# Three feed-forwards of a two-block model: who makes the low halves of the first six weight blocks, and when

## The reference, cut to what matters

```
def swiglu(h, w13, w2):
    gate, up = jnp.split(h @ w13, 2, axis=-1)
    return (jax.nn.silu(gate) * up) @ w2

x = x + 0.5 * swiglu(rms_norm(x, g), w13, w2)      # six times, D_FF = 2816
x = x + token_mixer(rms_norm(x, g), ...)           # pooling, HGRN, RWKV-7 and GLA heads, then y @ w_out
x = x + rglru_block(rms_norm(x, g), ...)           # conv, gates, linear recurrence, then y @ w_out
x = x + stick_breaking_block(rms_norm(x, g), ...)  # attention, then o @ w_o
```

## Time and profile before

| what | value |
|---|---|
| median of three runs | 1563.62 us |
| span of the profiled execution | 1561.3 us |
| TensorE, weight loads | 1536.0 us (98%), 1335.9 (86%) |
| VectorE, ScalarE, GpSimd | 1078.8 (69%), 776.3 (50%), 982.8 (63%) |
| mean DMA | 169 GB/s |

### The profile page before, as it was taken

One profiled execution on the slowest core, in us unless ns is written; L12 is line 12 of the kernel. 1 busy time (PEld: TensorE's weight loads), 2 busy tenths in 40 slices (PEclk: granted clock), 3 DMA queues, 4 the chain that ended last, 5 costly groups with the idle time before them and its releaser, 6 DMA issues.

```text
span 1561.3 us, 25169 instructions
## 1 busy us (share of the span) xinstructions
PE 1536.0 (98%) x9772; PEld 1335.9 (86%) x9772; DVE 1078.8 (69%) x1451; ACT 776.3 (50%) x1118; POOL 982.8 (63%) x1154
## 2 busy tenths in 40 slices
PE   9999999999999999999999999999999999999998
PEld 7888887887788888888998788888888888878887
DVE  7866555756886668976579886656776655688664
ACT  6454442023555465554666555455555454665542
POOL 7966520202886677876774886676977671288764
PEclk9999999999999999999999999999999999999999
DMA  8665533222465564565636466564465561336553
GB/s 294 204 195 184 187 109 109 75 90 97 166 210 188 169 199 158 191 202 183 195 132 189 145 210 190 168 223 139 156 224 181 166 229 55 134 121 222 182 167 120
DMA packets 107206, 263.69 MB, mean 169 GB/s; under 512 B 9168, under 2 KB 43088, under 8 KB 106960
## 3 DMA queue, kind: packets, MB, share of 16 engines
q1 hardware_dynamic: 107088, 262.09, 51.0%
HBM read 261.00 MB, written 1.05 MB: 168 GB/s over the span
## 4 chain that ended last, share of the span: by engine, by line
PE 83%; POOL 7%; DVE 6%; ACT 2%; issue 1%; DMA 0%; SPq 0%; DVEq 0%; ACTq 0%
PE ps L1739 38%; PE ps L1740 21%; POOL w_lo L543 7%; PE ps L1787 6%; PE ps L1742 4%; PE ps L1833 2%; PE ps L1771 2%; PE ps L1773 1%; PE ps L1772 1%; PE ps L1854 1%; PE ps L2046 1%; PE ps L1941 1%; DVE xn L1023 1%; PE ps L1803 1%; DVE arena L1680 1%
## 5 line engine op out<-in xcount | busy, mean ns | idle before, releaser
L543 POOL TENSOR_TENSOR w_lo<-raw,w_hi 128x256 fp32r<-128x256 f32 x1120 | 964.1, 895 | 463.0 <-ACT w_hi L625 460.1
L1739 PE MATMUL ps<-xn,w_hi 128*128 128x512 f32 x1848 | 662.0, 397 | 11.0 <-POOL w_lo L543 5.2
L625 ACT ACTIVATE w_hi<-raw 128x1024 fp32r<-128x1024 f32 (+1 forms) x518 | 477.7, 933 | 175.3 <-PE ps L1742 100.4
L1740 PE MATMUL ps<-xn,w_lo 128*128 128x256 f32 x2112 | 550.3, 280 | 0.0
L1739 PEld LDWEIGHTS ps<-xn,w_hi 128*128 128x128 f32 x1848 | 346.4, 187 | 94.3 <-POOL w_lo L543 8.4
L1740 PEld LDWEIGHTS ps<-xn,w_lo 128*128 128x128 f32 x2112 | 398.4, 189 | 16.8
L1739 PE MATMUL ps<-hid,w_hi 128*128 128x512 f32 x1008 | 363.4, 396 | 1.2 <-DVE w_lo L1015 1.2
L1015 DVE TENSOR_TENSOR w_lo<-raw,w_hi 128x512 fp32r<-128x512 f32 (+1 forms) x232 | 269.4, 1161 | 35.6 <-ACT w_hi L625 30.4
L1740 PE MATMUL ps<-hid,w_lo 128*128 128x256 f32 x1056 | 292.4, 281 | 0.0
L1739 PEld LDWEIGHTS ps<-hid,w_hi 128*128 128x128 f32 x1008 | 190.1, 189 | 42.5 <-issue 1.5
L1099 DVE TENSOR_TENSOR arena<-ps,low_part 128x512 f32<-128x512 f32 x132 | 90.8, 688 | 179.2 <-ACT low_part L716 179.0
(11 more groups left out here) (334 smaller groups left out, 1496.1 us busy)
## 6 DMA issues: line engine op xcount, KB each, us to landing
raw<-blocks SPq DMA_DIRECT2D x419, 512.0 KB, 3.6
raw<-blocks SPq DMA_DIRECT2D x144, 256.0 KB, 3.6
cst<-consts SPq DMA_DIRECT2D x1, 2358.0 KB, 14.9
x<-x_in SPq DMA_DIRECT2D x4, 256.0 KB, 5.4
out<-x SPq DMA_DIRECT2D x4, 256.0 KB, 3.3
cst<-consts SPq DMA_DIRECT2D x1, 109.0 KB, 2.1
```

The costliest lines, as they stand in the source:

```text
L543: ins = nc.gpsimd.tensor_tensor(w_lo[:, slot(n), piece], raw[:, slot(n), piece], w_hi[:, slot(n), piece], ALU.subtract)
L625: nc.scalar.activation(w_hi[:, slot(n), cols], raw[:, slot(n), cols], ACT.Copy)\
L1739: nc.tensor.matmul(where, hi, both.rearrange("p a t -> p (a t)"), start=opens, stop=False)
L1740: ins = nc.tensor.matmul(where[:, 0:SEQ], lo, high, start=False, stop=False)
```

## The change

In words: in front of `ffn_b`, `ffn_d` and `ffn_f` (`BEHIND_ROWS`) GpSimd makes the low halves of blocks 0, 1 and 5, VectorE those of 2 and 3 before its first sum of x and that of 4 behind the squares; VectorE's additions of squares move behind all sums of x and low halves. ScalarE has a norm of its own there: the high halves of blocks up to 3 (`ffn_b`) or 4 (`ffn_d`, `ffn_f`) are made ahead of the first sum, in the mixer those of 0 and 1 ahead of a wait; squares come one pair later, and the high halves up to block 5 right behind them. GpSimd takes the low halves of rows 4 and 5 of `lru_out` from VectorE. At the start there are 7 of the old unused products and 16 others in fp32r, for which VectorE fills a part of `hid` with ones. `ffn_a`, `ffn_c` and `ffn_e` keep their order.

```diff
-UNUSED_PRODUCTS = 11
+UNUSED_PRODUCTS = 7
+BEHIND_ROWS = {"ffn_b": "mix_out", "ffn_d": "lru_out", "ffn_f": "attn_out"}
+POOL_ROWS = (4, 5)
+def first_on_vector(phase):
+    return DVE_SPLITS if phase == "ffn_a" else (2, 3, 4) if phase in BEHIND_ROWS else ()
...
@@ GpSimd
+                if phase == "lru_out":
+                    for i in POOL_ROWS:
+                        lo(n0 + i)
...
-                    for n in range(n0, n0 + 2 * LEAD):
-                        if n not in DVE_SPLITS:
-                            lo(n)
+                    for i in range(2 * LEAD):
+                        if i not in first_on_vector(phase):
+                            lo(n0 + i)
@@ ScalarE
+            def norm_behind_rows(version, phase, gains):
+                n0 = FIRST[phase]
+                def square(a):
+                    nc.scalar.activation(squares(a, gains), pair_of_x(a), ACT.Square).then_inc(sq_ready, 1)
+                for a in range(4):
+                    act.wait_ge(x_ready, 4 * (version - 1) + a + 1)
+                    high_halves(gains, a)
+                    if a:
+                        square(a - 1)
+                square(3)
+                hi_until(n0 + 2 * LEAD - 1)
+                preload(ACT.Sqrt)
+                state["norms"] += 1
+                take_low(FFN_OF[gains], n0, 0)
...
@@ ScalarE, mixer_one
                 inverse_root(rms_r[:, :, :], bank(4), HD, const("gn_eps"), "rw_gn_root")
+                hi_until(FIRST["ffn_b"] + 1)
                 need(act, "on_done", 2)
                 inverse_root(norm_sb[:, 0, :], bank(6)[:, 0, :], G, const("norm_eps"), "on_root")
-                hi_until(FIRST["ffn_b"] + 2)
+                hi_until(FIRST["ffn_b"] + 3)
@@ ScalarE, lru and attention
-                hi_until(out_rows + 8 + 2)
+                hi_until(FIRST["ffn_d"] + 4)
...
-                hi_until(FIRST["ffn_f"] + 2)
+                hi_until(FIRST["ffn_f"] + 4)
@@ VectorE
+            def next_x(scale, gains, rows, following):
+                n0 = FIRST[following]
+                def add(a):
...
+                before, behind = first_on_vector(following)[:2], first_on_vector(following)[2:]
+                for i in before:
+                    lo(n0 + i)
+                add(0)
+                add(1)
+                low_halves(gains, 0)
+                add(2)
+                low_halves(gains, 1)
+                add(3)
+                low_halves(gains, 2)
+                low_halves(gains, 3)
+                for a in range(4):
+                    add_squares(a, gains)
+                for i in behind:
+                    lo(n0 + i)
                 sums_done[0] += 1
                 inverse_root(gains)
@@ VectorE, lru
                     y_low("lru_out", lru_gate, i)
-                    lo(FIRST["lru_out"] + i)
+                    if i not in POOL_ROWS:
+                        lo(FIRST["lru_out"] + i)
@@ VectorE, start
-            nc.vector.memset(low_part[:, :, :], 1.0).then_inc(ones_ready, 1)
+            nc.vector.memset(low_part[:, :, :], 1.0)
+            nc.vector.memset(hid[:, 0:2, :, :].bitcast(F32), 1.0).then_inc(ones_ready, 1)
@@ TensorE, start
+            unused_both = hid[:, 0, :, :].rearrange("p a t -> p (a t)")
+            for _ in range(4):
+                nc.tensor.matmul(ps[:, 7, 0:SEQ], hid[:, 0, 0, 0:P], hid[:, 0, 1, :], start=True, stop=True)
+            for _ in range(3):
+                nc.tensor.matmul(ps[:, 7, :], hid[:, 0, 0, 0:P], unused_both, start=True, stop=True)
+            for _ in range(3):
+                nc.tensor.matmul(ps[0:HD, 7, 0:SEQ], hid[:, 0, 0, 0:HD], hid[:, 0, 1, :], start=True, stop=True)
+            for _ in range(3):
+                nc.tensor.matmul(ps[:, 7, 0:SEQ], hid[0:HD, 0, 0, 0:P], hid[0:HD, 0, 1, :], start=True, stop=True)
+            unused_apart = hid[:, 0:2, :, :].rearrange("p c a t -> p (c a) t")[:, :, 0:P]
+            for _ in range(3):
+                nc.tensor.matmul(ps[:, 7, :], hid[:, 0, 0, 0:P], unused_apart, start=True, stop=True)
```

More of the change, by code:

```diff
@@ L636, in preload, with norm @@
                 chain(nc.scalar.activation(table[:, 0:4], table[:, 4:8], func))
-            def norm(version, gains, then=ACT.Silu, after=None, late=(), behind=None):
+            def norm(version, gains, then=ACT.Silu, after=None, behind=None):
                 for a in range(4):
@@ L678, in norm @@
                     preload(then)
+            def norm_behind_rows(version, phase, gains):
[12 more added lines that the diff above has]
+                take_low(FFN_OF[gains], n0, 0)
+                act.wait_ge(total_ready, state["norms"])
+                nc.scalar.activation(rms[:, :], ps[:, 3, 0:SEQ], ACT.Sqrt, scale=1.0 / D, bias=const("norm_eps"))\
+                    .then_inc(rms_ready, 1)
+                preload(ACT.Silu)
             def first_norm():
@@ L991, in _ @@
                 lambda: (act.wait_ge(const_loaded, 16), norm(1, "g_mix", ACT.Exp, after="ffn_a"), mixer_one()),
-                lambda: norm(2, "g_ffn_b", late=(0, FIRST["ffn_b"] + 3, FIRST["ffn_b"] + 4)),
+                lambda: norm_behind_rows(2, "ffn_b", "g_ffn_b"),
                 lambda: ffn(1, FIRST["ffn_b"]),
@@ L996, in _ @@
                 lambda: (norm(5, "g_lru", ACT.Exp, after="ffn_c", behind=FIRST["lru_in"] + 5), lru()),
-                lambda: (norm(6, "g_ffn_d", late=(0, FIRST["ffn_d"] + 3, FIRST["ffn_d"] + 4)), ffn(3, FIRST["ffn_d"])),
+                lambda: (norm_behind_rows(6, "ffn_d", "g_ffn_d"), ffn(3, FIRST["ffn_d"])),
                 lambda: (norm(7, "g_kv", None, after="ffn_d", behind=FIRST["kv"] + 5), shared_kv()),
@@ L1000, in _ @@
                 lambda: (norm(8, "g_attn", None, after="ffn_e", behind=FIRST["q_in"] + 5), attention()),
-                lambda: (norm(9, "g_ffn_f", late=(0, FIRST["ffn_f"] + 3, FIRST["ffn_f"] + 4)), ffn(5, FIRST["ffn_f"]), hi_until(end)),
+                lambda: (norm_behind_rows(9, "ffn_f", "g_ffn_f"), ffn(5, FIRST["ffn_f"]), hi_until(end)),
             ]
@@ L1039, in add_squares @@
                     ins.then_inc(sum_ready, 1)
[L1041 to L1058, removed]
+            def next_x(scale, gains, rows, following):
+                n0 = FIRST[following]
+                def add(a):
+                    if a < 3:
+                        v.wait_ge(acc_done, 3 * sums_done[0] + a + 1)
+                    else:
+                        v.wait_ge(used[slot(LAST[rows] - 1)], nth(LAST[rows] - 1))
+                    nc.vector.scalar_tensor_tensor(pair_of_x(a), ps[:, a, :], scale, pair_of_x(a), ALU.mult, ALU.add)\
+                        .then_inc(x_ready, 1)
+                    x_tiles[0] += 1
+                    v.wait_ge(x_ready, x_tiles[0])
+                before, behind = first_on_vector(following)[:2], first_on_vector(following)[2:]
[13 more added lines that the diff above has]
+                    lo(n0 + i)
                 sums_done[0] += 1
@@ L1713, in _ @@
                 lambda: whole_ffn(0, "ffn_a", "g_mix"),
-                lambda: (mixer_one(), end_sublayer(1.0, "mix_out", "g_ffn_b")),
+                lambda: (mixer_one(), end_sublayer("ffn_b", "g_ffn_b")),
                 lambda: whole_ffn(1, "ffn_b", "both"),
                 lambda: whole_ffn(2, "ffn_c", "g_lru", gain_x),
-                lambda: (lru(), end_sublayer(1.0, "lru_out", "g_ffn_d")),
+                lambda: (lru(), end_sublayer("ffn_d", "g_ffn_d")),
                 lambda: whole_ffn(3, "ffn_d", "g_kv"),
@@ L1720, in _ @@
                 lambda: whole_ffn(4, "ffn_e", "g_attn"),
-                lambda: (attention(), end_sublayer(1.0, "attn_out", "g_ffn_f")),
+                lambda: (attention(), end_sublayer("ffn_f", "g_ffn_f")),
                 lambda: whole_ffn(5, "ffn_f", None),
```

6 lines of the change are left out of this document (2 added, 4 removed).

## The result

The changed kernel took **1553.41 us** (median of five runs, 1553.14 to 1554.25) against 1563.33 us (five runs, 1563.08 to 1563.69): ratio 0.9937, interval 0.9926 to 0.9949. It is faster by 9.9 us, where 8.2 was forecast. The profiled execution spans 1551.3 us, 2.1 under that median.

A forecast was written before the change was run, and what follows sets the result against it. TensorE, busy 98% of 1561.3 us, was taken as the bound, with only its waits to win. -14.7 + 4.2 + 2.1 + 0.2 = -8.2 us gave a median of 1555.4 us, own range 1554.3 to 1557.0.

The forecast's parts named there:

- parts 1 and 2: Feed-forwards 2, 4 and 6: new boundary order and the sixth block ready earlier; together 14.7 us gained of 15.0.
- The price of a wait: TensorE's waits at the three boundaries: each costs 0.26 us more than its bracketed idle time, 4.7 us for 18 waits.
- the unlisted wait ahead of the fourth up tile: In each of feed-forwards 2, 4 and 6, a wait too short for the list: 0.40 us each, 1.2 in all.
- part 1: Boundary order: VectorE takes three blocks, squares go behind; a pair of tiles costs VectorE 1.6 us instead of 3.8.
- (3): LRU: two output rows move to GpSimd, whose eight pieces each stretch a VectorE operation by 0.52 us; 4.2 us lost.
- (4): Mixer of feed-forward 2: GpSimd's four pieces of a block meet the operations that make y; 2.1 us lost.
- (5): Kernel start: new unused products and second memset end at 10.0 us against 9.3, mostly taken up; 0.2 us lost.
- smaller new waits: Rival: scans not stretched, or GpSimd's pieces fall elsewhere; 1553.3 us, with none of the new waits 1548.9; chance 0.24.
- the likeliest case: The forecast itself: 8.2 us gained, median 1555.4 us, own range 1554.3 to 1557.0; chance 0.43.
- GpSimd still the bound: Rival: up blocks 4 and 5 still late in the feed-forwards' first steps; 3.9 us given back, 1559.3; chance 0.10.
- VectorE late at the sums: Rival: block halves delay the first sum of x; 3.3 us per boundary; chance 0.03 at full price, 0.11 at half.
- The clock falls: Rival: 4 us without products at the LRU's rows lowers TensorE's clock; about 2.3 us, 1557.7; chance 0.09.

The follow-up runs named there:

- the experiment: The changed kernel with the high half of the sixth block made only in the feed-forward's first step, behind the norm, as before the change: 1561.02 us.

## Why the prediction was right, and where it was off

- **Bound and gross gain (parts 1 and 2).** Predicted 14.7 us out of the three boundaries; measured 14.8. The price of a wait (its bracket and 0.26) and the unlisted wait ahead of the fourth up tile were both needed: brackets alone give 9.1. The sixth block's waits came out at 6.5 us in the table and 6.6 in the experiment.
- **The reason given in part 1 was half wrong.** I put 1.2 of the 3.8 us per pair down to the additions of squares between the sums. Their place does not matter (squares put back: 0.05). What made the pair long was GpSimd beside it: 1.91 instead of 0.88, 1.23 instead of 0.68. But in front of feed-forward 2 this was not what cost TensorE time in the new order: with all six blocks on GpSimd the step is the same (-0.06). Of the 14.8 us, 6.5 are shown to be the sixth block's; of the 8.3 up to the sums of squares (the table's first column and the new waits) the 2.7 of feed-forward 2 have no cause shown by a run.
- **(3) The LRU's rows** were right in place and kind, too large in size: 4.2 forecast, 3.1 measured. Eight operations were stretched, as said; each by 0.34 to 0.42 instead of the 0.52 read from a pair of low halves in the earlier trace rows. The forecast's other pair of rows, 1.23 and 1.65, gave 0.42, the size that came. Scans are no exception, the open point of the forecast: 0.69 became 1.10. The Trainium skill (SBUF — State Buffer, Who interferes with whom) says that a VectorE instruction with two SBUF inputs contends with a GpSimd instruction that reads SBUF, with no exception for scans; these rows agree (0.69 became 1.10). What I missed is that VectorE's relief, "counted" as a part of the gain, was all that the move bought: with both rows back the LRU's step is the same to 0.03.
- **(4) The mixer's y**: 2.1 forecast, 1.35 measured in the changed kernel, for the same reason (the scalings together, the addition and the product each grew by 0.4 to 0.5). The forecast had no gain from it, and none is shown.
- **(5) The start**: 0.2 forecast, +0.37 in one profile, +0.08 in the second of the same kernel. It is not resolved. Of its terms, the end of the unused products was forecast at 10.0; seven wide products took 6.28 us instead of 4.7, and the first product of feed-forward 1 starts at 11.63. It started at 9.33 before, but TensorE then waited for block halves (1.4 and 0.4 us in the list of 0:30); in the changed kernel that list has no wait of this kind, so most of the 2.3 us is taken up.
- **Sum.** 8.2 + 1.1 (LRU) + 0.75 (mixer) + 0.1 (gross) - 0.1 (start) = 10.0, the spans' difference; the median stood 2.1 above the span, not 2.3. The forecast was 2.0 too high for these reasons, the mis-sized term being the 0.52 us that an operation beside GpSimd was said to lose: 0.34 to 0.42 at the LRU, and at the mixer 1.35 for the four pieces together.
- **The rivals.** The result, 1553.4, is that of "smaller new waits" (1553.3), and outside the likeliest case's own range by 0.9. Its reason was only partly there: the pieces fell where forecast and stretched the scans, but by less. "GpSimd still the bound" did not occur: no wait on it is left. "VectorE late at the sums" occurs in small in front of feed-forward 2: the late load of the fourth block, which the forecast argued away, holds up the first sum of x, and TensorE's wait on it is 0.2 to 0.7 us with this order. The rival's price was 3.3 us at each boundary. **"The clock falls" occurs in some executions**: not in the first profile, in the second. Its price, forecast at 2.3, was 1.2 there. (The forecast's own rows, 22 products of 0.243 against 7.32, give 2.0.) That rival and the likeliest case are thus not exclusive, as I had treated them.

## What to carry to other kernels

Before handing a piece of work to an idle engine, look at what its neighbour does in that very window: a low half taken off VectorE saved its 1.65 us later and cost 0.4 for each operation beside it at once, and the wait only changed its name. When a wait cannot be removed, split it if you can: 2.8 us and more in one piece was followed by a fall of the clock in most profiles here, 2.0 us or less in none. And judge an edit by the marks of its own stage, not by the total, where stages elsewhere vary by a microsecond from one execution to the next.

## What the runs showed of the hardware that was not expected

- **After 2.9 us of idleness the clock fell in some executions and not in others.** Eight profiles have a wait of 2.8 to 2.9 us at the LRU's row 4. In six of them the granted clock fell behind it or in it (both changed rows late, the mixer's order back, the sixth block late, all on GpSimd, the old start, the changed kernel again), in two it stayed at 1.00. In the five without that wait, with 2.0 us or less at a time, it stayed at 1.00 there. Where it fell, the LRU's step was 1.0 to 2.4 us longer, other waits of the edit included. What decides is not shown: of the two profiles of the changed kernel, one has the fall.
- **GpSimd's unbroken run can hold up a VectorE operation until it ends**: 3.61 us for an operation that takes 0.48, while the pieces ran at 0.70; elsewhere the two engines alternate, 0.4 to 0.5 us lost to an operation. It is no accident of that execution. Every profile of this case, the kernel before included, has a case in front of feed-forward 3. Timelines of VectorE and of GpSimd, kernel before:

```profile
581.06 3.48 DVE L1023 SCALAR_TENSOR_TENSOR xn<-x,gain_both,xn 128x256 fp32r<-128x256 f32 x2 [0.66 <-ACT xn L705]
```

```profile
569.18 14.67 POOL L543 TENSOR_TENSOR w_lo<-raw,w_hi 128x256 fp32r<-128x256 f32 x20 [0.16 <-ACT w_hi L625]
```

  The first of these two low halves took 3.08 us, the second 0.47. The first ended at 584.14, 0.3 behind the end of GpSimd's run (583.85), which is also the distance at 1366.1 and 1365.82. No wait of TensorE comes of it there. Why some operations are held up and others alternate is open.
